# A table of constants made 32 columns narrower, in a two-block transformer kernel

## The reference

```
h = x
y = rmsnorm(h, ffn1_pre_g) * (1 + sc1) + sh1
h = h + 0.5 * g1 * rmsnorm(swiglu(y), ffn1_post_g)
y = rmsnorm(h, mix_pre_g) * (1 + sc2) + sh2
h = h + g2 * rmsnorm(token_mix(y), mix_post_g)
...                                     # a second FFN like the first
for i in range(2):                      # gla_mixer, then diff_mixer
    x = x + gate_t * mixer(rmsnorm(x) * (1 + scale_t) + shift_t)
    x = x + gate_c * (square(relu(h @ mlp_w1)) @ mlp_w2)
return rmsnorm(x, final_g)
```

## The kernel before

| tensor | start |
|---|---|
| `h_sb`, `yhi`, `ylo` | 16512, 32896, 49280 |
| `raw`, `whi`, `wlo` | 65664, 90240, 106624 |
| `cst` | 123008 |
| `msk`, `par`, `mod`, `crow` | 125856, 126880, 129248, 129920 |
| `tmps` (8 buffers, pitch 2064) | 134368 |
| `rs`, `hs` | 150880, 150944 |
| region of each block (`first`; `ffn1_y`, `ffn1_ahi0`; `mlp0_ahi0`; ...) | from 151168 |

## Time and profile before

### The profile page before, as it was taken

One profiled execution on the slowest core, in us unless ns is written; L12 is line 12 of the kernel. 1 busy time (PEld: TensorE's weight loads), 2 busy tenths in 40 slices (PEclk: granted clock), 3 DMA queues, 4 the chain that ended last, 5 costly groups with the idle time before them and its releaser, 6 DMA issues.

```text
span 2363.4 us, 27396 instructions
## 1 busy us (share of the span) xinstructions
PE 2305.3 (98%) x11040; PEld 1897.5 (80%) x11040; DVE 1336.5 (57%) x1985; ACT 846.3 (36%) x1286; POOL 210.2 (9%) x177
## 2 busy tenths in 40 slices
PE   8999999999999999999999999999999989999998
PEld 7888887777778888887787988888967768888887
DVE  7655548486357455548543566664566764644343
ACT  3322223424443322223723442322334453423221
POOL 0000003031023000003010100000121101000001
PEclk8999999999999999999999999999999999999999
DMA  8766632311211466642231256663221111443331
GB/s 313 249 202 203 199 121 73 108 40 41 73 61 55 121 217 205 199 121 73 68 101 52 72 178 218 211 209 110 66 82 54 54 45 56 150 127 96 98 98 36
DMA packets 81917, 287.01 MB, mean 121 GB/s; under 512 B 9088, under 2 KB 11520, under 8 KB 81792
## 3 DMA queue, kind: packets, MB, share of 16 engines
q1 hardware_dynamic: 80928, 283.43, 37.6%
q10 hardware_dynamic: 864, 1.84, 0.2%
HBM read 283.13 MB, written 2.10 MB: 121 GB/s over the span
## 4 chain that ended last, share of the span: by engine, by line
PE 86%; DVE 8%; ACT 3%; issue 1%; POOL 0%; DMA 0%; SPq 0%; DVEq 0%; ACTq 0%; POOLq 0%
PE bank L289 23%; PE bank L290 23%; PE bank L291 23%; DVE wlo L1611 2%; PE bank L506 1%; PE bank L426 1%; PE bank L452 1%; PE bank L427 1%; PE bank L428 1%; PE bank L447 1%; PE bank L448 1%; PE bank L557 1%; ACT whi L1013 1%; DVE attd L1991 1%; PE bank L339 1%
## 5 line engine op out<-in xcount | busy, mean ns | idle before, releaser
L1611 DVE TENSOR_TENSOR wlo<-raw,whi 128x1024 fp32r<-128x1024 f32 (+1 forms) x368 | 473.1, 1286 | 330.0 <-ACT whi L1013 329.5
L289 PE MATMUL bank<-yhi,whi 128*128 128x512 f32 (+1 forms) x1670 | 657.0, 393 | 0.5 <-DVE ylo L1967 0.5
L290 PE MATMUL bank<-ylo,whi 128*128 128x512 f32 (+1 forms) x1670 | 645.7, 387 | 0.0
L291 PE MATMUL bank<-yhi,wlo 128*128 128x512 f32 (+1 forms) x1670 | 645.5, 387 | 0.0
L1013 ACT ACTIVATE whi<-raw 128x1024 fp32r<-128x1024 f32 (+1 forms) x368 | 383.1, 1042 | 292.4 <-PE bank L291 247.3
L289 PEld LDWEIGHTS bank<-yhi,whi 128*128 128x128 f32 x1670 | 314.6, 188 | 83.0 <-issue 20.3
L291 PEld LDWEIGHTS bank<-yhi,wlo 128*128 128x128 f32 x1670 | 314.7, 188 | 64.3
L290 PEld LDWEIGHTS bank<-ylo,whi 128*128 128x128 f32 x1670 | 314.7, 188 | 61.8 <-issue 1.7
L289 PE MATMUL bank<-mlp_ahi,whi 128*128 128x512 f32 (+1 forms) x552 | 206.6, 374 | 0.0
L290 PE MATMUL bank<-mlp_alo,whi 128*128 128x512 f32 (+1 forms) x552 | 206.2, 374 | 0.0
L291 PE MATMUL bank<-mlp_ahi,wlo 128*128 128x512 f32 (+1 forms) x552 | 206.2, 374 | 0.0
(11 more groups left out here) (347 smaller groups left out, 2851.2 us busy)
## 6 DMA issues: line engine op xcount, KB each, us to landing
raw<-in_ada SPq DMA_DIRECT2D x152, 512.0 KB, 4.3
raw<-in_ffn_up SPq DMA_DIRECT2D x88, 512.0 KB, 4.4
raw<-in_mlp_up SPq DMA_DIRECT2D x64, 512.0 KB, 3.6
raw<-in_mlp_dn SPq DMA_DIRECT2D x64, 512.0 KB, 3.6
raw<-in_ffn_dn SPq DMA_DIRECT2D x32, 512.0 KB, 4.0
raw<-in_w_dqkv SPq DMA_DIRECT2D x24, 512.0 KB, 3.6
first<-in_ada SPq DMA_DIRECT2D x16, 512.0 KB, 14.9
raw<-in_ffn_dn SPq DMA_DIRECT2D x16, 384.0 KB, 3.6
```

What stands on the lines that cost most here:

```text
L289: e.matmul(out, wh, xh, start=first, stop=False)
L290: e.matmul(out, wh, xl, start=False, stop=False)
L291: mm = e.matmul(out, wl, xh, start=False, stop=last)
L1611: e.tensor_tensor(k.wlo[:, what % NW, 0:width], raw[:, 0:width], k.f(k.whi[:, what % NW, 0:width]), ALU.subtract).then_inc(*sig.up("wlo", ...
```

## The change

The width of the table of constants goes from 711 to 679 columns. The columns 679 to 710 are zeros that nothing reads. The arrays in DRAM and SBUF get narrower by 128 bytes per partition, and every SBUF tensor declared after `cst` starts 128 bytes lower.

```
-IDENT, ONES, PERM, CAUS, CNEG, INVF_C, EPS_C, HPI_C, SEL_C, QUAD_C, PAIR_C, NCONST = 0, 128, 256, 384, 512, 640, 641, 642, 643, 647, 655, 711
+IDENT, ONES, PERM, CAUS, CNEG, INVF_C, EPS_C, HPI_C, SEL_C, QUAD_C, PAIR_C, NCONST = 0, 128, 256, 384, 512, 640, 641, 642, 643, 647, 655, 679
```

## The result

| | before | after |
|---|---|---|
| median of five runs | 2362.7 us (2358.01 to 2365.17) | 2377.09 us (2372.65 to 2379.54) |
| the profiled execution, its span | 2365.17, 2363.4 us | 2377.69, 2375.9 us |
| mean granted TensorE clock | 0.985 | 0.986 |

The ratio is 1.0061, with a 95% interval of 1.0042 to 1.0081: 14.4 us slower, beyond the 7.1 us that I had set as the bound, and 10 us above the upper end of my range.

The account below looks back on a forecast made before the run. The prediction took the count of TensorE matmuls, 0.226 us each, as the bound, plus short places where something else leads. Terms 0 - 0.05 + 0 = -0.05 us gave 2362.6 us from the 2362.7 median, range 2358.0 to 2367.0.

Parts of the forecast that it names:

- the 7.1 us that I had set as the bound: Whole kernel: about what a measurement can tell from no change; 2355.6 to 2369.8 us counts as the same.
- Parts (1) and (2): Table of constants: dropped columns are never read, cost 0; its load, 16,384 bytes shorter, saves 0.05 us, at most 0.22.
- the 0.05 us: Load of the constants at the start: saving from 16,384 fewer bytes at 352 GB/s.
- Part (3), VectorE, ScalarE, weights: Tensors behind the constants, 128 bytes lower: VectorE, ScalarE and weight loads would not care about the new remainders; 0 us.
- TensorE, moving operand: Moving reads of hidden tiles: placement taken to cost 0, bounded at 1 ns each over 2712 reads, 2.7 us either way.
- Realigned tiles are read more slowly: Rival, hidden-tile matmuls: tiles at multiples of 512 clash, each of 2712 pays; 2369.8 us at 2.6 ns; chance 0.015 slower, 0.015 faster.
- threshold of 2.6 ns: Hidden-tile matmuls: extra time each from which slower reads decide the outcome, 7.1 us / 2712.
- Loads get faster because their targets are aligned: Rival, loads of `first` and `crow` at the start: worth at most 0.8 us, giving 2361.8, still the same; chance 0.03.
- The clock's falls: Rival, TensorE's low-clock stretches land differently: 2369.8 us or more, or about 2354; chance 0.03 faster, 0.03 slower.
- My 0.47 us per us: Low-clock stretch at the start: cost of each us that the clock's rise at 41.2 us comes later.
- The edit moves nothing: Rival, whole placement: padded some other way, time 2362.7 us; chance 0.88 together with the forecast of no measurable change.
- What would show it: Signs in the profile after: 27396 instructions, `cst` 339.5 KB, L289 to L291 at 389 ns, L1931 at 693 ns.

Follow-up runs that it names:

- region_back: Changed kernel plus 128 bytes of padding directly ahead of the blocks' region, putting it back where before had it; 2361.57 us, ratio 0.9999 to before.
- all_up: Kernel before plus 128 bytes of padding ahead of everything, so all tensors move and all distances stay; 2361.71 us, ratio 1.0 to before.
- map2: Separate matmul-only kernel varying weight columns, moving columns and types at distances 0, 64, 128, 192; 226.6 ns at 0, 232.4 at 128 for full width.
- region_up: Kernel before, wide table kept, plus 128 bytes of padding directly ahead of the blocks' region; 2376.02 us, ratio 1.0063 to before.
- ahead_up: Changed kernel plus 128 bytes of padding ahead of everything: hidden tiles at 128, weights at 0 modulo 256; 2378.39 us, ratio 1.0073 to before.
- region_p64: Kernel before plus 64 bytes of padding ahead of the blocks' region, hidden tiles at distance 64 from the weights; 2364.62 us, ratio 1.0015 to before.
- region_256: Kernel before plus 256 bytes of padding ahead of the blocks' region, distance 0 modulo 256; 2362.63 us, ratio 0.9999 to before.
- weights_up: Changed kernel plus 128 bytes of padding between `ylo` and `raw`, hidden and y tiles all at distance 128 from the weights; 2402.51 us, ratio 1.0173 to before.
- map: Separate matmul-only kernel, weights at eight starts against moving tiles at sixteen; mean interval 226.7 ns at distance 0, 233.3 at 128 (modulo 256).
- triples: Separate kernel running the three-product pattern over 512 placements of `wlo`, `xhi`, `xlo` against `whi`; 226.7 ns at one remainder, mean 232.0, worst 236.

## Why the prediction was wrong, by its own steps

*Parts (1) and (2), the dropped columns and the shorter load:* right. 27396 instructions, `cst` at 339.5 KB. The shorter load landed after 5.2 us in place of 4.9 and the wait for it was 6.4 us in place of 6.1, in one execution each, so the 0.05 us is far below what a start varies by, and region_back, which has this load too, stands at 0.9999.

*Part (3), VectorE, ScalarE, weights:* right. L1931 at 692 ns, busy times equal to 0.2 us, L305 at 106 to 110 ns.

*Part (3), "TensorE, moving operand":* this is the step that failed. I bounded the reads at 1 ns each, 2.7 us in all, took 0, and gave the rival *Realigned tiles are read more slowly* a chance of 0.015 on the slow side. The runs showed 6.6 ns on each of the 2472 full-width hidden matmuls, 16.4 us, and nothing on the 240 half-width ones. The rival had the place right, and its threshold of 2.6 ns is passed; what it had wrong is the quantity. "If the hidden tiles at multiples of 512 clash with something" takes the start of the tile as the cause, and all_up has the tiles at 0 and no loss. It is the distance to the weights, modulo 256. The bound had two faults. It came from rows of other types: L882 and L500 are plain fp32, for which map2 finds no effect at any of four distances, so they could not have shown one; L305 loads 32 columns of plain fp32 weights. And it leaned on "every row that varies a placement", when for the matmuls at stake no row varied it: `yhi`, `ffn_ahi` and `mlp_ahi` all lay at distance 0, the one place where nothing shows. I had written that these rows tell "nothing of 0" and still set the bound without them. No row of before gives a price; an honest bound would have been open above, and 3 ns each (8.1 us over 2712) was enough to turn the forecast into slower.

The Trainium skill would not have warned: its page "SBUF — State Buffer", section "Who interferes with whom", gives TensorE two independent read ports, one for the moving operand and one for the weight loads, and says that "PE and ACT never wait on anyone". The second statement is about other engines. The first does not fit the runs as far as it would mean that the two reads have nothing to do with each other: the interval is 226.7 or 233.3 ns by nothing but where the two operands lie to each other, and here the measurement decides. That the two ports are what collides is not shown.

*Loads get faster because their targets are aligned:* right that it is worth nothing in the kernel's time, and the mechanism is small at best.

```profile
first<-in_ada SPq DMA_DIRECT2D x16, 512.0 KB, 14.5
```

The median landing goes from 14.9 us to 14.5, 3%, the size of the estimate that the prediction draws from the Trainium skill's "DMA: Bandwidth & Descriptors". That page tells of bytes fetched ahead of an unaligned start, and these are targets. The other traces lean the same way: 14.5, 14.6 and 14.3 us where `first` starts at a multiple of 256 (after, region_up, all_up), 14.9, 15.0, 14.6, 15.0, 15.0 and 14.9 where it does not (before, region_back, ahead_up, region_p64, region_256, weights_up). It stays open whether the alignment does it, and region_up and all_up gain no time by it.

*The clock's falls:* not the cause; in the profiled execution they even hide part of the loss. The mean is 0.986 against 0.985. The low stretch at the start is 20.5 us long in both traces and only lies later, from 22.6 to 43.1 us in place of 20.8 to 41.3. My 0.47 us per us was for a stretch that gets longer, so it has no use here. The lag behind before is 0.56 us at 80 us. It grows in the stretches that read hidden tiles, 2.8 us at 352, 6.2 at 419, 13.3 at 1705, but some 2 us of the 6.2 are a longer fall of the clock around 400 us:

```profile
399.80:403.10 3.30, 3.30 (x16) 3.26 (x17) 2.41 (x9) 0.30 (x1) 0.00 (x0) 0.50 0.00 0
```
```profile
401.60:411.70 10.10, 9.71 (x40) 8.17 (x39) 5.75 (x15) 2.23 (x4) 1.66 (x2) 0.50 0.07 28
```

(Before, then after, with the columns of the earlier trace rows.) From 1705 to 2000 us it is before that has more of the lower clock, by 10.2 us, and the lag falls to 8.3. It ends at 12.7.

*The edit moves nothing:* wrong; a pad of the same 128 bytes undoes all that it did.

*Slips in the working:* the three matmuls are 69 of the 86%, four fifths and not three quarters; and 7.1 us below 2362.7 is 2355.6, not "about 2354". Neither touches the forecast.

*What would show it:* "An L289 of 392 ns on `mlp_ahi` with 389 on `yhi` would prove me wrong on the reads" came out to the number, 392 at the median with `yhi` at 389.

What stays open is the mechanism: which read holds up which, if that is what it is. The map gives the rule for tiles and weights that keep one distance (period 256), but neither a matmul's own weights nor the next one's explain the mixed pairs. The alternation of 229.2 and 237.6 ns inside a pair of equal placement, the two rhythms in weights_up and the slow start of the placement in triples say that the starts of its own operands don't settle a matmul's interval; what came before it has a part.

## What to carry to other kernels

A change of a table's width is a change of place for everything declared behind it. With fp32r matmuls of 512 columns keep the moving tiles and the weight tiles at one remainder modulo 256 bytes, and hold them there by a pad that says so: here each of 2472 matmuls off it cost 2 to 7 ns of 227, in after together the price of 72 matmuls. And rows that all share one value of a quantity put no bound on what another value costs, nor do rows of another type of operand.

## What the runs showed of the hardware

- At the full clock an fp32r matmul of 128x128 by 128x512 takes up 226.7 ns when its operands have the same start modulo 256, and 229.0 to 233.9 ns on average at other distances; bf16 takes 215.8 ns at each of four distances. (Full clock, back to back, in map and map2.)
- A half-width one (256 columns) is the other way round, if anything: 120.0 ns at distance 0 and 117.7 to 118.8 elsewhere; in the kernel 121.1 before and 120.1 after.
- In a sequence of three products no placement of 512 is faster than the equal one, 226.7 ns against a mean of 232.0. One other (128, 0, 160 past `whi`) settles at the same 226.7 ns after seven slower matmuls.
- The interval is not a function of the placement alone: at distance 128 the hidden matmuls of weights_up ran at 233.3 ns in two stretches and at 232.4 in eight.
- With fewer than 128 weight columns distance 0 loses its advantage (96 columns: 229.9 ns, and 228.6 at distance 192), and with 480 or 448 moving columns it is not the fastest either (216.6 ns at 0, 215.7 at 192; 202.5 at 0, 200.1 at 64).
- Executions of nearly the same program differ in how long TensorE has its lower clock: 54.7 us (region_back) to 74.7 us (before) in the profiled executions.
